# Summing pairs of gathered rows in 32x32 array tiles over four PSUM banks, with a new plan of where the rows stand

## The reference, cut to what matters

```
def one(xs):                                  # 128 tokens
    q = (xs @ wq).reshape(128, 8, 2, 128)     # 8 heads, 2 halves
    s1, s2 = scores of each half against 128 keys; top 16 of each
    top, j = lax.top_k(all 256 sums of the two top lists, 16)
    eid = ids of the 16 chosen experts        # per token and head
    g = softmax(top)
    a = gelu(einsum('nd,nhjd->nhj', xs, u[eid]))
    return einsum('nhj,nhjd->nd', g * a, v[eid])
```

## Time and profile before

| | us |
|---|---|
| median of 3 runs | 3636.49 (3633.03 to 3644.66) |
| the profiled execution, its own time | 3632.81 |
| its span, first to last instruction | 3630.8 |
| PE busy | 2895.9 (80%) |
| DVE busy | 1752.8 (48%) |
| ACT busy | 1113.7 (31%) |
| POOL busy | 833.3 (23%) |

### The profile page before, as it was taken

How to read it: one execution, slowest core, us unless ns; L and a number is a source line. 1 busy time by engine, 2 the same in 40 slices (tenths; PEclk the granted TensorE clock), 3 DMA queues, 4 the chain that set the end, 5 groups by cost and what they waited for, 6 DMA issues and landing times.

```text
span 3630.8 us, 42719 instructions
## 1 busy us (share of the span) xinstructions
PE 2895.9 (80%) x16338; PEld 1815.1 (50%) x16338; DVE 1752.8 (48%) x4345; ACT 1113.7 (31%) x3085; POOL 833.3 (23%) x772
## 2 busy tenths in 40 slices
PE   7899998888998999887865556589999875556565
PEld 5677887554555666654421111267888751111111
DVE  1323012447666555344767766414310146666664
ACT  1322102243555454224433322231310122333232
POOL 0000000223333333122334434200000014444442
PEclk9999999989999999989977777789999987776767
DMA  8554442888998999777899999831234279999997
GB/s 313 232 202 169 151 151 85 312 325 323 362 363 312 421 412 421 284 298 303 308 377 417 414 417 417 361 116 47 93 128 153 71 288 413 413 418 413 410 409 288
DMA packets 151107, 1071.77 MB, mean 295 GB/s; under 512 B 16564, under 2 KB 18228, under 8 KB 22520
## 3 DMA queue, kind: packets, MB, share of 16 engines
q0 software_dynamic: 110592, 805.36, 55.1%
q1 hardware_dynamic: 40312, 263.69, 19.2%
HBM read 1067.93 MB, written 1.05 MB: 294 GB/s over the span
## 4 chain that ended last, share of the span: by engine, by line
PE 56%; DMA 24%; DVE 9%; ACT 7%; issue 3%; POOL 1%; DVEq 0%; ACTq 0%; SPq 0%; POOLq 0%
PE bank L372 42%; DMA ring<-in_experts,eid 21%; PE bank L386 11%; DVE ring L1317 4%; DMA weights<-in_quads 3%; POOL ring L1734 1%; PE bank L465 1%; ACT topk_work L872 1%; ACT topk_work L865 1%; ACT topk_work L862 1%; DVE state L1498 1%; ACT L862 1%; ACT h_even L925 0%; ACT L956 0%; PE bank L399 0%
## 5 line engine op out<-in xcount | busy, mean ns | idle before, releaser
L1734 POOL DMA_INDIRECT ring<-in_experts,eid x768 | 833.1, 1085 | 2759.3 <-PE bank L386 1464.0
L386 PE MATMUL bank<-ring,topk_work 64*64 64x512 f32 x6144 | 982.6, 768 | 539.1 <-ACT topk_work L872 535.0
L1317 DVE CUSTOM_DVE_ANT_0 ring<-ring,h2tok 128x1024 f32<-128x1024 f32 x768 | 937.4, 1224 | 556.1 <-DMA ring<-in_experts,eid 552.1
L386 PEld LDWEIGHTS bank<-ring,topk_work 64*64 64x64 f32 x6144 | 235.9, 159 | 1191.9 <-ACT topk_work L872 894.6
L862 ACT ACTIVATE topk_work<-topk_work 128x2 f32<-128x2 f32 x384 | 78.0, 203 | 1135.1 <-DVE topk_work L1317 1134.5
L372 PE MATMUL bank<-h_even,weights 128*128 128x256 f32 (+1 forms) x1168 | 278.7, 399 | 43.3 <-DMA weights<-in_quads 28.2
L372 PEld LDWEIGHTS bank<-h_even,weights 128*128 128x128 f32 (+1 forms) x1168 | 224.3, 194 | 102.3 <-DMA weights<-in_quads 30.2
L872 ACT ACTIVATE topk_work<-const,topk_work 128x64 f32<-128x64 f32 x768 | 225.7, 341 | 0.4 <-PE bank L386 0.2
L372 PE MATMUL bank<-h_odd,weights 128*128 128x256 f32 (+1 forms) x896 | 212.0, 393 | 17.2 <-DMA weights<-in_quads 15.5
L372 PEld LDWEIGHTS bank<-h_odd,weights 128*128 128x128 f32 (+1 forms) x896 | 169.5, 193 | 70.7 <-issue 24.8
L372 PE MATMUL bank<-h_even,ring 128*128 128x256 f32 (+1 forms) x896 | 200.2, 382 | 5.2 <-ACT h_even L925 4.6
(11 more groups left out here) (217 smaller groups left out, 3231.2 us busy)
## 6 DMA issues: line engine op xcount, KB each, us to landing
weights<-in_quads SPq DMA_DIRECT2D x137, 1024.0 KB, 8.0
ring<-in_quads SPq DMA_DIRECT2D x98, 1024.0 KB, 4.8
ring<-in_experts,eid POOLq DMA_INDIRECT x768, 8.9
weights<-in_quads SPq DMA_DIRECT2D x7, 768.0 KB, 6.4
ring<-in_quads SPq DMA_DIRECT2D x5, 768.0 KB, 6.4
weights<-in_quads SPq DMA_DIRECT2D x12, 256.0 KB, 2.9
xT<-in_xT SPq DMA_DIRECT2D x1, 2048.0 KB, 10.9
out<-h_even SPq DMA_DIRECT2D x1, 1024.0 KB, 4.5
```

The lines of the kernel that those rows point to most:

```text
L386: x = nc.tensor.matmul(acc[g][out, :], diag[mine, J % 4, :], ring[mine, J % RING, D + h * 512:D + (h + 1) * 512], start=first, stop=J % TI ...
L1317: v.tensor_tensor_reduce(row, row, h2tok[:, u // UNITS % 2, :], 1.0, 0.0, ALU.mult, ALU.add, dots[:, u % 2, j:j + 1]).then_inc(S["dot_done ...
L1734: pool.indirect_dma_start(ring[:, J % RING, :], None, d["experts"], bass.IndirectOffsetOnAxis(eid[:, u % 2, j:j + 1], 0)).then_inc(gathere ...
```

## The change

The block size `BLK` goes from 64 to 32. A row is now eight matmuls of 32 by 32 with 512 columns: four blocks g of 32 tokens, two halves h. Block g has bank `SUM_BANKS[g]`, one of four; the even row of a pair lies on partitions 0 to 63 of it and the odd row on 64 to 127. So the 16 matmuls of a pair stand on 16 different tiles of the array (4 row groups by 4 column groups), where the four matmuls of each row stood on the same four tiles before. PE now waits for both diagonals before the first matmul of a pair. `tile_sum` adds the two partition halves as it turns them, with a matrix `pick` that has two ones in each column; it has 32 matmuls where it had 16, and `tile_out` has two copies each for DVE and ACT, which wait until the sum of the tile before has been read.

Own work has four banks (`MIXER_BANKS`) in passes 1 and 2 and in all `queries`, and eight in the rest of passes 0 and 3. In the linear attention of pass 1 the second half of the state update now stands behind the output that it used to precede. The plan charges 0.5 for a row and 2.3 for a load.

```diff
-BLK = 64
+BLK = 32
-BANKS = 6
+BANKS = 8
+MIXER_BANKS, SUM_BANKS = (0, 1, 2, 3), (4, 5, 6, 7)
-PER_LOAD, LANDS, LAG = 2.5, 2.0, 5.0
+PER_LOAD, LANDS, LAG = 2.3, 2.0, 5.0
...
             def job(*key, loose=False):
-                n = len(job_log)
+                which = cur["banks"]
+                b = which[(which.index(cur["bank"]) + 1) % len(which)] if cur["bank"] in which else which[0]
+                cur["bank"] = b
                 job_log.append(key)
-                if n >= BANKS:
-                    pe.wait_ge(*at("evicted", *job_log[n - BANKS]))
+                bank_log[key] = b
+                if b in last_in:
+                    pe.wait_ge(*at("evicted", *last_in[b]))
+                last_in[b] = key
...
             def row_pair(n):
+                k, m = divmod(n, TILE_PAIRS)
+                if m == 0:
+                    for b in SUM_BANKS:
+                        if b in last_in:
+                            pe.wait_ge(*at("evicted", *last_in[b]))
+                pe.wait_ge(S["diag_ready"], 2 * n + 2)
                 for J in (2 * n, 2 * n + 1):
-                    k, first = J // TILE_ROWS, J % TILE_ROWS == 0
-                    if first and J:
-                        for g in range(2):
-                            pe.wait_ge(*at("evicted", "acc", k - 1, g))
-                    pe.wait_ge(S["diag_ready"], J + 1)
                     for h in range(2):
-                        out = slice(h * BLK, (h + 1) * BLK)
-                        for g in range(2):
+                        out = slice(J % 2 * 64 + h * BLK, J % 2 * 64 + (h + 1) * BLK)
+                        for g in range(4):
                             mine = slice(g * BLK, (g + 1) * BLK)
                             x = nc.tensor.matmul(acc[g][out, :], diag[mine, J % 4, :],
                                                  ring[mine, J % RING, D + h * 512:D + (h + 1) * 512],
...
             def tile_sum(k):
-                for g in range(2):
+                for g in range(4):
                     pe.wait_ge(*at("evicted", "acc", k, g))
-                for g in range(2):
-                    b = job("yt", k, g, loose=True)
+                for h in range(2):
+                    b = job("yt", k, h, loose=True)
                     for c in range(4):
-                        for h in range(2):
...
+                        for g in range(4):
+                            x = nc.tensor.matmul(b[:, c * P + g * BLK:c * P + (g + 1) * BLK],
+                                                 sums(k, g)[:, c * P:(c + 1) * P], pick[:, h, :], start=True, stop=True)
...
                 for J in (2 * n, 2 * n + 1):
-                    plan.now += 0.95
+                    plan.now += 0.5
...
                     for m in range(2):
+                        if m and p.full and p.beside is not None:
+                            breathe(2.0)
+                            pe.wait_ge(*at("evicted", "s", n, u, 0, 1))
+                            of_state(1)
+                            breathe(1.5)
                         for g in range(2):
                             b = job("s", n, u, m, g)
...
+                banks(*range(BANKS) if p.beside is None else MIXER_BANKS)
...
             def tile_out(k):
                 dve.wait_ge(S["row_used"], (k + 1) * TILE_ROWS)
-                copy_out(sums(k, 0), acc[0][:, :], "acc", k, 0)
+                if k:
+                    dve.wait_ge(*at("full", "yt", k - 1, 1))
+                for g in (0, 2):
+                    copy_out(sums(k, g), acc[g][:, :], "acc", k, g)
```

More of the change, by code:

```diff
@@ L138, in build @@
     placed, full_at = logs["placed"], logs["full"]
-    quads_of = logs["quads"]
+    quads_of, bank_no = logs["quads"], logs["bank"]
     ctx = ExitStack()
@@ L200, in gate_buf @@
             return lent[:, 1] if n == 0 else VVc
-        ps = [ctx.enter_context(nc.psum_tensor(f"bank{n}", [P, 512], F32)) for n in range(BANKS + 2)]
-        acc = ps[BANKS:BANKS + 2]
+        ps = [ctx.enter_context(nc.psum_tensor(f"bank{n}", [P, 512], F32)) for n in range(BANKS)]
+        acc = [ps[b] for b in SUM_BANKS]
         tri = const[:, C_TRI:C_TRI + 256].rearrange("p (d t) -> p d t", d=2)
@@ L229, in build @@
         pqT = AB
-        work = sb("topk_work", [P, 1840])
+        work = sb("topk_work", [P, 1200])
         pos = [0]
@@ L329, in _ @@
         def _(pe):
-            cur = {"q": None, "slots": (), "turn": 0, "next": 0, "limit": 0, "pass": 0}
+            cur = {"q": None, "slots": (), "turn": 0, "next": 0, "limit": 0, "pass": 0,
+                   "banks": tuple(range(BANKS)), "bank": None}
+            last_in = {}
             uses = [0] * (FIXED + EXTRA)
@@ L539, in outputs @@
                             full(x, "s", n, u, m, g)
-                    if p.full:
-                        breathe(2.0)
+                    if p.full and p.beside is None:
                         pe.wait_ge(*at("evicted", "s", n, u, 0, 1))
@@ L827, in _ @@
                         slots(*range(FIXED))
+                    banks(*MIXER_BANKS)
                     queries(p)
@@ L884, in tile_out @@
                 act.wait_ge(S["row_used"], (k + 1) * TILE_ROWS)
-                copy_out(sums(k, 1), acc[1][:, :], "acc", k, 1)
+                if k:
+                    act.wait_ge(*at("full", "yt", k - 1, 1))
+                for g in (1, 3):
+                    copy_out(sums(k, g), acc[g][:, :], "acc", k, g)
             def rows_until(n):
@@ L1738, in build @@
         logs["jobs"], logs["quads"], logs["placed"], logs["full"] = job_log, quad_log, placed_now, full_now
+        logs["bank"] = bank_log
 LEADS = (0, 2 * 2 * UNITS)
@@ L1788, in constants @@
     out[:, C_BLK:C_BLK + BLK] = (p[:, None] % BLK) == np.arange(BLK)[None, :]
+    for h in range(2):
+        out[:, C_SEL + h * BLK:C_SEL + (h + 1) * BLK] = ((p[:, None] // BLK % 2 == h)
+                                                         & (p[:, None] % BLK == np.arange(BLK)[None, :]))
     band = np.zeros((len(WINDOWS), 256, 256), np.float32)
@@ L1875 @@
     arrays = layout({k: _np.asarray(v) for k, v in inputs.items()})
-    count, logs = None, {"jobs": [], "quads": [], "placed": {}, "full": {}}
+    count, logs = None, {"jobs": [], "quads": [], "placed": {}, "full": {}, "bank": {}}
     for _ in range(3):
```

32 lines of the change are left out of this document (19 added, 13 removed).

## The result

The changed kernel takes 3698.23 us (median of 4 runs, 3691.52 to 3704.98) against 3636.89 for the kernel before (4 runs, 3633.03 to 3644.66): 1.016 times the time, with a 95% interval of 1.0139 to 1.0182. It is slower, where 3558 was forecast. The profiled execution took 3697.76, its span is 3695.8.

The account below looks back on a forecast made before the run. PE was held the nearer bound beside own work (the third stretch also DMA), gathers the bound of the tails. 3632.8 - 115 + 10 + 8 + 8 + 6 + 4 + 3 = 3554.8, plus 3.7: forecast 3558, 8-in-10 range 3510 to 3620.

Parts of the forecast that it names:

- A pair on PE, 1.0 for 1.87: Rows' matmuls on PE: 16 tiles run at once, so a pair at full clock takes 1.0 us instead of 1.87.
- Rival 3: Rows' pairs beside own work: column groups run one behind the other, making the kernel slower; decides from 1.68 us; chance 0.08.
- rival 2: Rows' pairs: the pair is not halved (1.55 to 1.68 us), no change in time, 3622 to 3644; chance 0.07.
- A to D: Four consecutive stretches, 629 to 1786 us, rows beside own work: together 1042 us instead of 1157, 115 less before charges.
- C bound by its bytes: Third of the four stretches: PE would need 259 us, but 116 MB need 278 at 418 GB/s, so 278.
- The two tile sums in B and D cost 3.8 us more each: Tile sums in the second and fourth stretch: 32 matmuls for 16, bound by weight loads, 3.8 us more each.
- the two tails of rows are bound by the gathers, and no faster PE shortens them: 1786 to 2348 and 2990 to 3606 us, almost only rows: DMA share 0.98 and 1.00; last tail stays 616.
- The clock, 6 us: Stretches beside own work: lower PE busy shares cost a few hundredths of clock in the third, 0.01 elsewhere: 6 us.
- Idle time, kept "at first", with 10 us for rows and 16 for banks: Stretches beside own work: PE's idle 42, 28, 9, 62 us kept; added 10 for row waits, 8 and 8 for banks.
- D, 281.: Fourth stretch: 232 - 28 + 11 + 4 + 62 = 281 us, with 11 more pairs, against 247 for its bytes.
- Rival 1: Waits eat more: rows, banks and clock cost 60 to 90 us instead of 32, time 3585 to 3620; chance 0.25.
- The signs: Wrong if a pair stays over 1.5 us, eviction waits exceed 30, or DMA in first two stretches stays 321 and 347.

Follow-up runs that it names:

- c_release: The kernel before, with both ring slots of a pair freed only after the second row, each row waiting for its own diagonal: 3744.87 us, ratio 1.0302.
- a_oldplan: The changed kernel with the plan's old costs (2.5 for a load, 0.95 for a row): 3727.91 us, ratio 1.0257 to the kernel before.
- b_banks4: The kernel before with four banks for own work in passes 1 and 2 and all queries, and the moved state update: 3653.28 us, ratio 1.0048.

## Why the prediction was wrong, point by point

The forecast missed by 140 us and by its sign. Its last sum has a slip of 2 us: 3632.8 - 115 + 39 is 3556.8, not 3554.8. By its own steps:

- **A pair on PE, 1.0 for 1.87.** Right: 1.08 measured at full clock, and 2.02 at half clock. No row and no run shows the 1.0, which was the author's estimate. Rival 3 (column groups one behind the other) and rival 2 (not halved) are out; the rows' busy time in A to D fell by 119.5 us, where 143 were forecast. Most of the difference is half clock: 147 pairs at 1.08 would be 159 us, and they are busy 185. By the windows A has 1 pair fewer, B 5, C 5 and D 10 more, where 2, 3, 6 and 11 were counted; that is a few us at most.
- **C bound by its bytes.** Right: 285.8 us at 407 to 409 GB/s, with PE idle 24.7 us, 9%, as "PE idle 10%" had it; forecast 278 without charges.
- **"The two tile sums in B and D cost 3.8 us more each".** This step failed, and it is the largest term that a run shows. Twice the matmuls was right, but each record takes 213 ns instead of 118, because the block runs at half clock. At full clock, with 114 ns a record, the two would have cost 3.5 us more each, as charged. With the charges before pass 3 and at the end, 14.6 us stood for it; the sums grew by 55.5, and a cheap sum in their place is worth 45 to 51 us of the whole time. Two of the six sums, those within the tails, had no charge at all, since the tails were held to have slack.
- **"the two tails of rows are bound by the gathers, and no faster PE shortens them".** True, but the step drew from it that no change of PE lengthens them, and that failed by 40 and 37 us. PE sits in the loop that frees the slots, as c_release shows. The short sum takes back 12 and 13 us, fillers that raise the clock another 17 and 17, and two more pairs account for some 10 in the first.
- **The clock, 6 us.** Mis-sized. The rule used (busy share to clock, from the earlier trace rows) did not carry over: it had 0.91 for 79 and 85% busy, and now A is granted 0.88 at 81% busy, B 0.91 at 84, D 0.82 at 76, and the last tail 0.50 at 42%. Half of the PE busy time that lies under a half clock is what the clock costs PE (a pair takes 1.87 us at full clock and 3.69 at half); summed over A to D it is 47 us before and 94.5 after, so the charge should have been some 48, of which some 12 lie in the two sums. That the busy shares would fall was in the step; what it costs was not.
- **Idle time, kept "at first", with 10 us for rows and 16 for banks.** PE is idle 195 us in A to D instead of 140: 16 of the 55 more are C's, as forecast, and 39 stand against 26 charged. The waits of PE, us in total, times, longest: first in 650:1200 of the changed kernel (before: the earlier trace rows), then in 1450:1777 (before, nearly the same stretch: the earlier trace rows).

```profile
PE bank L401 <- ACT topk_work L894: 23.5, 14, 6.7
PE bank L386 <- DMA weights<-in_quads: 17.0, 7, 6.5
PE bank L605 <- ACT gla_work L1132: 14.6, 7, 3.7
PE bank L386 <- DVE state L1528: 7.7, 2, 4.7
```

```profile
PE bank L401 <- ACT topk_work L894: 30.2, 10, 8.1
PE bank L386 <- DMA weights<-in_quads: 17.9, 4, 8.5
PE bank L386 <- ACT h_even L951: 7.0, 1, 7.0
```

- The waits for rows fell from 40.9 to 23.5 in the first window, and in the second they are 30.2 where 24.3 stood. With the old plan in the changed kernel (a_oldplan) they are 54.8 in the first, so the new plan is what keeps PE from rows that have not landed. In their place PE waits 17.0 us for weights (9.5 before) and 14.6 for an exponential of latent attention (L605), the wait that was charged with 8 for four banks. Four banks alone don't make it: in b_banks4 it is 2.6 in the same window.
- **D, 281.** 332. Eleven more pairs were charged; besides, 9 us of slower sum and some 28 us more lost to half clock (45.3 against 17.5), which overlap by some 6. A to C gained 36 us together, where 103 were forecast, and D took 34 of them back.
- **The rivals.** Rival 1 had the right kind (rows, banks and clock eat the gain) and too small a price: it let 60 to 90 us go, where 180 went (the stretches were to give 115, and the span grew by 65), the sums and the tails with it. None of the range's bounds let a term rise because the clock falls.
- **The signs.** Of the three by which the prediction was to be wrong, the pair over 1.5 us did not come, and waits for evictions are not told apart from others in the rows above. The third came: the DMA rate in A and B stays at 320 and 326 GB/s, against 321 and 347 before. PE's shorter pairs did not make the gathers faster there.

## What to carry to other kernels

When PE's share of busy time falls, price the stretch again at a lower clock before you book the saving: the last tail here was granted 0.73 with PE busy 59% and 0.50 with 42%, and a pair that is 42% shorter took some 120 us of busy time away and won 13 against the same kernel with long pairs. Count a long block of 32-column matmuls behind full 128x128 fp32 weights at half clock (64 records took 12.9 to 13.9 us here, 213 ns each once the clock had fallen), and turn it round so that the small matrix is the weights (25.3 us for the six sums in place of 81.5). Count also how many pairs a new plan leaves for each stretch before you compare the stretches. An engine that isn't the bound may still free the bound's buffers (c_release: tails 46 and 62 us longer); ask of each edit whether buffers now come free later, or all at once.

## What the runs showed of the hardware that was not expected

- Useless matmuls made two kernels faster, by 21 and 15 us by their ratios: the last tail was granted 0.82 of full clock with PE busy 66%, and 0.51 with 39%.
- A block that keeps PE busy all the time, with 64 records of 128x32 under 128x128 fp32 weights, fell to half clock inside itself: 114 ns a record at first, then 213. The same sum in 32 records of 64 columns stayed at full clock in five of six, 118 ns each.
- Sixteen 32x32 fp32 tiles in flight gave 1.08 us for 32 records of 512 columns, eight tiles 1.87, as do four of 64x64. Twice the number of records and of weight loads (32 each a pair for 16) cost nothing beside that: 1.87 us both times.
- Freeing the first of two slots one row later made tails of 512 and 626 us 46 and 62 us longer, at 373 and 368 GB/s instead of 407 and 404.
